# A hybrid decoder layer on eight cores: rotary scores on halves of the TensorE array, and queries on partitions behind the softmax

## What is computed

```python
q_nope, q_rope = q_all[..., :A_NOPE], q_all[..., A_NOPE:]      # 128 and 64 channels
q_rope = apply_rope(q_rope, cos[:, :, None, :], sin[:, :, None, :])
...
k_rope = apply_rope(a_kr, cos, sin)                     # (B,S,A_ROPE), shared by heads
qa = jnp.concatenate([q_nope, q_rope], axis=-1)
...
s = jnp.einsum('bhqd,bshd->bhqs', qi, k).astype(jnp.float32) * scale
s = jnp.where(k_pos[None, :] <= q_pos[:, None], s, -jnp.inf)
p = jax.nn.softmax(s, axis=-1)
return jnp.einsum('bhqs,bshd->bqhd', p.astype(v.dtype), v)
...
ha = causal_block_attention(qa, ka, v_a) * jax.nn.silu(a_z)
```

## Time and profile before

| | us |
|---|---|
| median of 3 runs | 2753.42 |
| lowest, highest | 2752.53, 3109.31 |
| the profiled execution | 2744.32 |
| span of its slowest core (core 2) | 2743.3 |
| spans of the 8 cores | 2733.9 to 2743.3 |
| granted TensorE clock, mean by core | 0.995 to 0.997 |

### The profile page before, as it was taken

How to read it: one execution, slowest core, us unless ns; L and a number is a source line. 1 busy time by engine, 2 the same in 40 slices (tenths; PEclk the granted TensorE clock), 3 DMA queues, 4 the chain that set the end, 5 groups by cost and what they waited for, 6 DMA issues and landing times.

```text
span 2743.3 us, 41380 instructions; the slowest of 8 cores (2733.9 to 2743.3 us)
## 1 busy us (share of the span) xinstructions
PE 2672.1 (97%) x13767; PEld 1327.7 (48%) x14037; DVE 1056.1 (38%) x1790; ACT 903.8 (33%) x1745; POOL 621.5 (23%) x924
## 2 busy tenths in 40 slices
PE   7999999999999999999999999999999999999998
PEld 3544444564547544455555444444444444444444
DVE  6646375458484567354424311111111111111433
ACT  5532365446463456354544211111111111110212
POOL 0003100101201212277760122222222222221000
PEclk9999999999999999999999999999999999999999
DMA  8546623514435322456545744444575545447562
GB/s 252 131 127 164 188 64 102 124 46 106 94 70 124 90 57 62 95 152 158 156 109 154 165 77 75 79 77 73 78 169 92 92 75 80 77 74 136 170 228 85
DMA packets 141250, 310.27 MB, mean 113 GB/s; under 512 B 14385, under 2 KB 72561, under 8 KB 134001
## 3 DMA queue, kind: packets, MB, share of 16 engines
q0 software_dynamic: 42048, 134.27, 29.9%
q1 hardware_dynamic: 94674, 160.23, 18.3%
q10 hardware_dynamic: 4320, 13.11, 1.5%
HBM read 369.12 MB, written 72.68 MB: 161 GB/s over the span
## 4 chain that ended last, share of the span: by engine, by line
PE 89%; DMA 6%; ACT 2%; issue 1%; DVE 1%; SPq 0%; POOL 0%; ACTq 0%; DVEq 0%; POOLq 0%
PE bk L290 88%; DMA xt<-x 1%; DMA xo<-x 1%; DMA cq<-CQT 1%; DMA kr<-KRT 1%; DMA maskf<-mask 1%; SPq L135 0%; DMA QNT<-ob 0%; DMA HMT<-hm 0%; ACT L294 0%; ACT junk L294 0%; PE bk L514 0%; DMA mb<-BH 0%; PE bk L1226 0%; PE bk L1180 0%
## 5 line engine op out<-in xcount | busy, mean ns | idle before, releaser
L290 PE MATMUL bk<-hT,wg 128*128 128x512 bf16 x2986 | 675.0, 379 | 4.5
L290 PE MATMUL bk<-w,hT 128*128 128x512 bf16 (+1 forms) x3016 | 594.3, 344 | 15.3 <-DMA w<-wA 5.3
L290 PE MATMUL bk<-hT,w 128*128 128x512 bf16 x2061 | 487.1, 381 | 2.9
L290 PEld LDWEIGHTS bk<-hT,wg 128*128 128x128 bf16 x3072 | 300.4, 98 | 360.2
L290 PEld LDWEIGHTS bk<-w,hT 128*128 128x128 bf16 x3072 | 297.6, 98 | 256.5 <-issue 20.3
L294 ACT ACTIVATE sh<-bk 128x512 f32<-128x512 f32 x184 | 109.9, 597 | 849.5 <-PE bk L290 849.5
L290 PE MATMUL bk<-hb,wb 128*128 128x512 bf16 x1530 | 345.6, 379 | 0.3
L290 PEld LDWEIGHTS bk<-hT,w 128*128 128x128 bf16 x2112 | 206.2, 98 | 229.7 <-issue 4.2
L310 DVE SCALAR_TENSOR_TENSOR tm<-sh,bk 128x512 f32<-128x512 f32 x124 | 85.3, 688 | 558.8 <-PE bk L290 557.4
L290 PEld LDWEIGHTS bk<-hb,wb 128*128 128x128 bf16 x1536 | 150.3, 98 | 181.0
L303 DVE TENSOR_TENSOR den<-den,Pa 128x512 f32<-128x512 f32 (+3 forms) x288 | 180.4, 626 | 120.2 <-ACT Pa L294 109.6
(11 more groups left out here) (181 smaller groups left out, 2492.6 us busy)
## 6 DMA issues: line engine op xcount, KB each, us to landing
wg<-wGB POOLq DMA_DIRECT2D x96, 512.0 KB, 5.3
w<-wA POOLq DMA_DIRECT2D x48, 516.0 KB, 8.4
wb<-wGB POOLq DMA_DIRECT2D x96, 256.0 KB, 3.9
xt<-x SPq DMA_DIRECT2D x16, 1024.0 KB, 13.2
xo<-x SPq DMA_DIRECT2D x16, 1024.0 KB, 7.8
out<-xo SPq DMA_DIRECT2D x15, 1024.0 KB, 7.7
wo<-wOUT POOLq DMA_DIRECT2D x4, 2048.0 KB, 18.9
w<-wA POOLq DMA_DIRECT2D x16, 500.0 KB, 8.9
```

The lines of the kernel that those rows point to most:

```text
L290: fw.op("pe", lambda e: e.matmul(bk[o] if not isinstance(o, bass.AP) else o, lhsT=lhsT, rhs=rhs, start=start, stop=stop), reads=reads, wri ...
```

## The change

In MLA's scores, `kr` is now one tile with the 64 rotary rows twice, in rows 0 to 63 and again in 64 to 127, and `qr` is loaded for each head in the same manner (four DMAs of 32 rows). `emit_S` takes two key blocks at once: two plain matmuls, then two rotary matmuls, the first on rows 0 to 63 of the array and the second on rows 64 to 127, into two banks of PSUM; the built program gives both a tile size of 64 by 128. The product with the values has 128 queries of `Pa` as weights and the values moving, so that queries lie on partitions. The values have a further column of 2.0, whose result is twice the sum of the exponentials. `den`, `hia`, `loa`, `twob` and `rba` are gone. `fin_half` takes reciprocals of two columns and multiplies by value and gate in one instruction for each 128 queries; four transposes and a copy bring the result back to channels on partitions. The gate is computed with tokens on partitions (`AZ`), stored in four pieces per head and loaded in quarters. The output is in two banks, `PO`, which every query block uses again.

Besides: the tiles of `ob` have two halves, each with its own dependences; queries are stored by halves. The HMT stores go from SyncE's queue to ScalarE's; the load of the mLSTM's gate stands in another place; waiting pieces in `mlstm_gen` and `c_gen` have other lengths. At the end the residual tiles are loaded first, then the gain and, after the third of them has landed, `wo3`.

```diff
-    AZT_d = dscr("AZT", [1024, S])
+    AZ_d = dscr("AZ", [8, 128, 16, 128])
...
-    VA_d = dscr("VA", [8, 128, 16, 128])
+    VA_d = dscr("VA", [8, 128, 16, 130])
...
+            ob = Ring(tiles("ob", 6, [128, 2080], BF16, n=2))
...
+            def half(o, tb):
+                return ([], [o.rs[tb // 2]]) if tb % 2 else ([o.rs[tb // 2]], [])
...
+                fw.op("pool", lambda e: e.memset(o[:].rearrange("p (h t c) -> p h t c", h=8, t=2)[:, :, :, 128:130], 2.0), writes=o.rs)
...
+                    if tb % 2:
+                        c = slice(tb * 512 - 512, tb * 512 + 512)
+                        for ci in range(2):
+                            hh = 2 * pr + ci
+                            fw.dma("sp", QNT_d[hh * 128:(hh + 1) * 128, c], o3[ci][:, c], reads=[o3[ci].rs[tb // 2]], accs=[dr("QNT", hh)])
+                        fw.dma("sp", QRT_d[pr * 128:(pr + 1) * 128, c], o3[2][:, c], reads=[o3[2].rs[tb // 2]], accs=[dr("QRT", pr)])
...
-            krs = tiles("kr", 2, [128, S], BF16, top=True)
-            qns = tiles("qn", 2, [128, S], BF16, top=True)
-            qrs = tiles("qr", 2, [128, S], BF16, top=True)
-            kns = tiles("kn", 2, [128, S], BF16, top=True)
-            vxs = tiles("vx", 1, [128, 16, 128], BF16, top=True)
-            for i in range(2):
-                fw.op("dve", lambda e: e.memset(krs[i][:], 0.0), writes=[krs[i].r])
-                for lo in (32 * i, 64 + 32 * i):
-                    fw.dma("sp", krs[i][lo:lo + 32, :], KRT_d[lo:lo + 32, :], reads=[dr("KRT"), krs[i].r] if lo == 32 * i else [dr("KRT")], accs=[krs[i].r])
+            kr = mem.alloc("kr", [128, S], BF16, top=True)
+            qns = tiles("qn", 1, [128, S], BF16, top=True)
+            qrs = tiles("qr", 1, [128, S], BF16, top=True)
+            kns = tiles("kn", 1, [128, S], BF16, top=True)
+            vxs = tiles("vx", 1, [128, 16, 130], BF16, top=True)
+            for lo, src in ((0, 0), (32, 64), (64, 32), (96, 96)):
+                fw.dma("sp", kr[lo:lo + 32, :], KRT_d[src:src + 32, :], reads=[dr("KRT")], accs=[kr.r])
...
+                pr = h // 2
+                for g in range(4):
+                    src = pr * 128 + 64 * (g % 2) + 32 * i
+                    fw.dma("sp", qrs[i][32 * g:32 * g + 32, :], QRT_d[src:src + 32, :], reads=[dr("QRT", pr)], writes=[qrs[i].r] if g == 0 else [], accs=[qrs[i].r] if g else [])
...
-            SBk, POk, DNk = Ring(SB[0:2] + SB[5:6]), Ring(SB[2:4]), SB[4]
...
+            SBk, PO = Ring(SB[0:2] + SB[4:6]), SB[2:4]
...
-            def finish(h, qb, acc, po, r_po):
-                dn, r_dn = DNk
-                hi, lo, u, rb = his.next(), los.next(), us.next(), rbs.next()
-                cols = slice(qb * 512, (qb + 1) * 512)
-                az = azs[h % 2]
-
+            def fin_half(h, qb, hb_, az, hq):
+                po, r_po = PO[hb_]
+                rd = rds.next()
+                pv = po[:, 0:260].rearrange("p (b c) -> p b c", b=2)
+                fw.op("dve", lambda e: e.reciprocal(out=rd[:], in_=pv[:, :, 128:129].rearrange("p b c -> p (b c)")), reads=[r_po], writes=[rd.r])
+                for j in range(2):
+                    b = 2 * hb_ + j
+                    stt(hq[:, b, :], pv[:, j, 0:128], rd[:, j:j + 1], az[:, b, :], ALU.mult, ALU.mult, [r_po, rd.r, az.r], [hq.r] if b == 0 else [], [hq.r] if b else [])
+
+            def finish(h, qb, hq):
                 def f1():
-                    copy("dve", hi[:], acc[:], [acc.r], [hi.r])
-                    tt("pool", lo[:], acc[:], hi[:], ALU.subtract, [acc.r, hi.r], [lo.r])
-                    tt("dve", u[:], po[:, 0:512], az[:, cols], ALU.mult, [r_po, az.r], [u.r])
-
-                def f2():
-                    mm(dn, r_dn, (slice(None), slice(None)), twob[:], hi[:], True, False, [hi.r, RM])
-                    mm(dn, r_dn, (slice(None), slice(None)), twob[:], lo[:], False, True, [lo.r, RM])
-
-                def f3():
-                    act(rb[:], dn[:], AF.Ln, [r_dn], [rb.r])
-                    act(rb[:], rb[:], AF.Exp, [rb.r], [rb.r], scale=-1.0)
-
-                def f4():
+                    bt, r_bt = SBk.next()
+                    btb = b16(bt, 8)
+                    for b in range(4):
+                        fw.op("pe", lambda e: e.transpose(out=btb[:, b, :], in_=hq[:, b, :], identity=identb[:]), reads=[hq.r, RC], writes=[r_bt])
                     o = has.next()
-                    tt("dve", o[:], u[:], rb[:], ALU.mult, [u.r, rb.r], [o.r])
+                    copy("dve", o[:].rearrange("p (b c) -> p b c", b=4), btb[:, 0:4, :], [r_bt], [o.r])
                     fw.dma("sp", HAT_d[qb // 2, :, h, (qb % 2) * 512:(qb % 2) * 512 + 512], o[:], reads=[o.r], accs=[dr("HAT", qb // 2)])
-                later(1, f1)
-                later(4, f2)
-                later(5, f3)
-                later(7, f4)
-
-            yield ("need", "AZT0")
-            loads_az(0)
+                later(3, f1)
...
+                    yield ("need", "AZ%d%d" % (h // 4, qb))
+                    az, hq = azs.next(), hqs.next()
+                    fw.dma("sp", az[:], AZ_d[h, :, 4 * qb:4 * qb + 4, :], reads=[dr("AZ", h // 4, qb)], writes=[az.r])
...
-                        q_lo = max(kt, 4 * qb)
-                        n = (4 * qb + 4 - q_lo) * 128
-                        q0 = q_lo * 128
-                        kc_ = slice(kt * 128, (kt + 1) * 128)
-                        bs, r_bs = SBk.next()
-                        mm(bs, r_bs, (slice(None), slice(0, n)), kn[:, kc_], qn[:, q0:q0 + n], True, False, [kn.r, qn.r])
-                        dg = kt >= 4 * qb
-                        mm(bs, r_bs, (slice(None), slice(0, n)), kr[:, kc_], qr[:, q0:q0 + n], False, not dg, [kr.r, qr.r])
-                        if dg:
-                            mm(bs, r_bs, (slice(None), slice(0, 128)), identb[:], mneg[:], False, True, [RC, mneg.r])
-                        p = Ps.next()
-                        act(p[:, 0:n], bs[:, 0:n], AF.Exp, [r_bs], [p.r], scale=SC)
-                        if kt == 0:
-                            copy("dve", acc[:], p[:], [p.r], [acc.r])
-                        else:
-                            o = 512 - n
-                            tt("dve", acc[:, o:512], acc[:, o:512], p[:, 0:n], ALU.add, [acc.r, p.r], [acc.r])
-                        return p, n
-
-                    q = [emit_S(0), emit_S(1)]
+                        prs = []
+                        for j in range(2):
+                            k = kt + j
+                            n = (4 * qb + 4 - max(k, 4 * qb)) * 128
+                            prs.append((k, n, slice(4 * qb * 128 + 512 - n, 4 * qb * 128 + 512), slice(k * 128, (k + 1) * 128), SBk.next()))
+                        for k, n, qc, kc_, (bs, r_bs) in prs:
+                            mm(bs, r_bs, (slice(None), slice(0, n)), kn[:, kc_], qn[:, qc], True, False, [kn.r, qn.r])
+                        for j, (k, n, qc, kc_, (bs, r_bs)) in enumerate(prs):
+                            hf = slice(64 * j, 64 * j + 64)
+                            mm(bs, r_bs, (slice(None), slice(0, n)), kr[hf, kc_], qr[hf, qc], False, k < 4 * qb, [kr.r, qr.r])
+                        if kt >= 4 * qb:
+                            for k, n, qc, kc_, (bs, r_bs) in prs:
+                                mm(bs, r_bs, (slice(None), slice(0, 128)), identb[:], mneg[:], False, True, [RC, mneg.r])
+                        res = []
+                        for k, n, qc, kc_, (bs, r_bs) in prs:
+                            p = Ps.next()
+                            act(p[:, 0:n], bs[:, 0:n], AF.Exp, [r_bs], [p.r], scale=SC)
+                            res.append((p, n))
+                        return res
+
+                    q = emit_S(0)
                     tick()
-                    yield 4 * MM
+                    yield 3 * MM
                     for kt in range(nkt):
-                        if kt + 2 < nkt:
-                            q.append(emit_S(kt + 2))
+                        if kt % 2 == 0 and kt + 2 < nkt:
+                            q += emit_S(kt + 2)
                         p, n = q.pop(0)
-                        mm(po, r_po, (slice(None), slice(512 - n, 512)), vx[:, kt, :], p[:, 0:n], kt == 0, kt == nkt - 1, [vx.r, p.r])
+                        b0 = 4 - n // 128
+                        for b in range(b0, 4):
+                            po, r_po = PO[b // 2]
+                            c = (b % 2) * 130
+                            mm(po, r_po, (slice(None), slice(c, c + 129)), p[:, (b - b0) * 128:(b - b0 + 1) * 128], vx[:, kt, 0:129], kt == 0 and b % 2 == 0, kt == 4 * qb + 1 + 2 * (b // 2) and b % 2 == 1, [vx.r, p.r])
+                        if kt == 4 * qb + 1 or kt == nkt - 1:
+                            fin_half(h, qb, 0 if kt < nkt - 1 else 1, az, hq)
                         tick()
-                        yield 3 * MM * n / 512
-                    finish(h, qb, acc, po, r_po)
+                        yield 2.5 * MM * n / 512
```

(16 more changed lines are left out.)

82 lines of the change are left out of this document (32 added, 50 removed).

## The result

The changed kernel is slower by about 0.9%: four executions of it took 2773.52, 2775.38, 2777.46 and 2785.12 us, two of the kernel before 2752.53 and 2753.42 us. The ratio is 1.009, 95% interval 1.0052 to 1.0129. That is about 25 us more, where the forecast was 35.7 us less. The range did not hold it. In half of the first four executions of the changed kernel one die had a lower clock, which makes their median 2882 us; such executions are left out of every time and ratio here.

The account below looks back on a forecast made before the run. PE bounds the kernel: its matmul columns plus its idle time. Columns -31.3, switching +8.6, waits that go -18, waits that come +5 make -35.7 us: median 2753.4 becomes 2717.7, range 2694 to 2763.

Parts of the forecast that it names:

- Columns: PE's matmul columns: rotary pairs -27.6 us, product with values +2.9, exponential sums -13.8, transposes back +7.2; -31.3 in all.
- Switching the array: PE changing its division around each rotary pair: 0.054 us once per pair, +8.6 us, with ends 0 and 52.
- rival 2: Each change of PE's division drains the array: 52.5 us, not 8.6; 2762 us; decides from 138 ns; chance 0.12.
- Waits that go: PE's waits for `ob`, `hm`, `Pa`, `hmt`, `xo` and clock dips shrink or vanish: -18 us, ends 8 and 23.
- hm: PE's 3.2 us wait for the copy to `hm` goes, as the HMT store moves to ScalarE's queue.
- xo: PE's wait of 1.8 us for `xo`, at the end of the kernel, goes.
- ob: PE's 3.4 us wait for ScalarE's copy to `ob` goes, with `kr` fills gone and stores by halves.
- Pa: PE's 6.2 us of waits for `Pa` in seven places shrink with VectorE's and ScalarE's work; some stay.
- (d): PE's wait of 2.3 us for POOL's `hmt` goes because the piece before it is longer.
- Waits that come: Bank reads at query block ends, covered unless DVE is in a convolution, and `az` loads: +5 us, between 0 and 14.
- rival 3: DVE's wait for `az` holds up two banks: 3.4 us plus a 2 us dip per head; 2756 us; chance 0.10.

Follow-up runs that it names:

- experiment 12: 8 with three banks in turn for MLA's output and three for its scores, instead of two and four: 0.9936 to the kernel before.
- Experiment 6: The changed kernel with both rotary matmuls of a pair on rows 0 to 63, so they cannot overlap: 1.0213 to the kernel before.
- (2): The kernel before with only the pitch of VA's rows changed, 512 bytes written at a pitch of 520: 1.009 to the kernel before.
- (1): The changed kernel with 144 instead of 130 columns per block of values, store rows of 576 bytes: 1.0045 to the kernel before.
- experiment 11: 10 with the cross-attention stream's waiting pieces as before (4 and 4): 0.9954 to the kernel before.
- 10: The kernel before with the moves alone (ob halves, HMT queue, gate load, waiting pieces, end order), MLA's arithmetic unchanged: 1.0004 to the kernel before.
- 7: The changed kernel with 576-byte store rows of values and the rotary matmuls on all 128 rows: 1.0026 to the kernel before.
- 8: 7 with branch C's two waiting pieces as in the kernel before (4 and 4 instead of 8 and 1): 0.9981 to the kernel before.
- experiment 9: 7 with 6 instead of 3 units of the main stream at the start of each query block: 1.0037 to the kernel before.

## Why the prediction was wrong, point by point

Four terms failed. The pitch of VA was put at nothing and cost 12 to 25 us. Switching was put at 8.6 and cost 31.8. Of the waits, branch C's longer piece was counted as a gain and cost 8 to 14, and VectorE's lateness at the banks, behind a convolution or a late gate, cost 13.6 us where 5 were put down.

**Columns.** Right. Two rotary matmuls overlap, and the product steps at 0.057. The sum of experiment 12 (below) agrees with the rest of the columns.

**"Switching the array", +8.6 us.** The mechanism was named, the size was not: 31.8 us. I took the one step behind a float transpose with 64 columns of weights, 0.054 us once per pair, because rows 6 was the nearest row. The real price comes twice, 0.096 in and 0.103 out. The upper end of 52 held it, and rival 2 had its point of decision at 138 ns per change; the 100 ns measured are below that. So this term, 23 us too small, took more than all that the halves bring (27.6) but did not alone turn the result. Experiment 6 shows that it does not depend on overlap.

The Trainium skill (TensorEngine Tiling (Array Packing), Key Properties) says that changing the mode drains TensorE. By the runs a change costs 0.10 us, where 0.164 is what I had worked out for a full drain, so the rule spoke on the right side, at some 60% of that price.

**What was not in the sum: the pitch of VA.** The diff showed its rows at 130 columns for 128, and I priced nothing for it, since the bytes rise by 1.6%. It cost 25 us put into the kernel before (2) and 12 taken out of the changed one (1). Most of the difference is that of the slowest core: by the mean of the cores it is 22 and 16. The slowest core of 1 waited 7.9 us for one `az`, which made PE's waits for `hqa` 14.9 us against 11.3, and that of 2 had the long waits for `hm`. The 6 us left are open; in 2 the loads of the values also took longer (15.1 us for `vx` against 8.8). Beside the price of the changes this is the largest single thing missed.

**"Waits that go", -18 us.** About right for the moves that I priced: experiment 11, which has all of them but branch C's, gave -12.6. `hm` and `xo` went, `ob` and `Pa` only in part. In the changed kernel `Pa` did fall from 6.2 to 2.1, which experiments 10 and 11 show not to come from the moves; that it is VectorE's and ScalarE's lighter load is argued. But (d), `hmt`, was wrong: I counted a longer piece as a gain of 2.3 us, and the two numbers of `c_gen` cost 9 to 12 (7 against 8) and 14 us (10 against 11), 8 and 10 by the mean of the cores. The loads of `cz` arrive late for four of the products instead of two. The rows show why a small shift is enough: it puts the first of these loads behind a burst of weight and `hb` loads instead of ahead of it (experiments 8 and 11).

**"Waits that come", +5 us.** Too small: 11.3 us of PE's time for `hqa`, 2.3 more for a wait behind `az`, and the third bank gave 12 back. There are two causes. I had written that the piece is covered "unless DVE is in the middle of a convolution". It is, in four of the seven places (7.3 us): in the changed kernel three convolution products stand ahead on VectorE, and PE waits 2.3 us for the last `hqa`.

```profile
652.46 2.46 DVE L310 SCALAR_TENSOR_TENSOR y<-pre,cw,y 128x512 f32<-128x512 f32 x3 [0.26 <-DVE pre L840]
...
655.71 0.61 DVE L310 SCALAR_TENSOR_TENSOR hqa<-bk,rda,az 128x128 bf16<-128x128 f32 x2
...
656.47 0.27 PE L290 MATMUL bk<-vxb,Pa 128*128 128x129 bf16 x2 [2.30 <-DVE hqa L310]
```

The other cause is rival 3's, the load of `az`. VectorE waited for it 13.1 us in all:

```profile
L310 DVE SCALAR_TENSOR_TENSOR hqa<-bk,rda,az 128x128 bf16<-128x128 f32 x128 | 39.1, 346 | 21.8 <-DMA az<-AZ 13.1 <-DVE rda L1004 5.3
```

5.8 us of that ended at 331 us in the first head, 4.2 at 460 in the second, where the load had stood behind the seven loads of the next head and took 13.5 us to land, and 0.8 and 2.3 came later. PE lost 2.3 us by the first and 2.6 and 1.1, the longest of its waits for `hqa`, by the second: 6.0 in all, and in the same two heads 8.2 in experiment 1 and 7.3 in 7. Rival 3 as I stated it, one such wait in each head, did not happen, but its mechanism did, in two heads of eight, and in experiment 9 it cost PE 22.6 us.

**The ledger.** Against the forecast the result is 61 us too high. Switching 23, pitch 12 to 25, branch C 9 to 14, waits that come 9, the moves 5 short, less 4 for `Pa`: 54 to 72. By the mean of the cores, with pitch 16 to 22, branch C 8 to 10 and the moves 8 short, it is 60 to 68. From the other end, the means of 8, 7, 1 and the change are steps of one chain: -5.4, then 7.8 for C, 6.6 for the halves and 16.0 for the pitch, 25.0 in all, as measured. Experiment 12 has no division, pitch or C's shift, and the waits for `hqa` nearly gone. By my columns it should give 2.9 - 13.8 + 7.2 = -3.7, with the moves of experiment 11 (-12.6) -16.3 us; measured -17.6.

**The range** was too narrow at the upper end because it took in only ends of terms that I had listed. The misses all lay on one side, and the four times lie 11 to 22 us over the top. I had written that the forecast is wrong if PE's idle time moves by more than 25 us; it moved by 21, so this sign did not catch the miss. The busy time moved by 10 more: the columns and the gaps of the changes cancel (-31.3 + 31.8), and what is left is the time at the lower clock, by the estimate above 11 us.

## What to carry to other kernels

Price a change of TensorE's division at 0.1 us each way: with one pair of 512 columns between two changes the halves only break even, and with less they lose, so put many tiled matmuls between two changes, or pad with zeros to all rows. If the diff touches the shape of a tensor in DRAM, look at the pitch of its rows and at the landing times of its stores before anything else; eight more bytes per row here cost as much as the sums that were saved on PE. When a step's output bank is read by a busy VectorE queue, look at what else that queue stands behind (here a convolution and the load of a gate), and give the output a third bank before moving pieces about. When a wait names an engine, follow it back until it ends at work or at a DMA; and when two kernels differ by 10 us, compare the mean of the cores as well as the slowest.
